# Half of the first layer's output projection moved from behind the HGRN heads to between their levels

## What is computed

```python
proj = hn @ w_in_even[j]
u, q_b, f_b, i_b, g_b = jnp.split(proj, [...], axis=-1)
y_a = s5_mixer(u, ...)                       # (B, L, 512): state space layer and GLU
y_b = hgrn2_mixer(q_b, f_b, i_b, g_b, ...)   # (B, L, 512): 4 heads of 128
h = h + jnp.concatenate([y_a, y_b], axis=-1) @ w_out_even[j]
hn = rms_norm(h, mlp_norm[i])
h = h + jnp.square(jax.nn.relu(hn @ w_mlp_in[i])) @ w_mlp_out[i]
```

## Time and profile before

| | us |
|---|---|
| median of 3 runs | 2602.95 |
| lowest, highest | 2598.78, 2605.69 |
| the profiled execution's own time | 2599.74 |
| its span in the profile | 2598.0 |

### The profile page before, as it was taken

One profiled execution on the slowest core, in us unless ns is written; L12 is line 12 of the kernel. 1 busy time (PEld: TensorE's weight loads), 2 busy tenths in 40 slices (PEclk: granted clock), 3 DMA queues, 4 the chain that ended last, 5 costly groups with the idle time before them and its releaser, 6 DMA issues.

```text
span 2598.0 us, 32798 instructions
## 1 busy us (share of the span) xinstructions
PE 2464.0 (95%) x13054; PEld 1998.5 (77%) x13054; DVE 1191.4 (46%) x1229; ACT 548.1 (21%) x850; POOL 833.8 (32%) x493
## 2 busy tenths in 40 slices
PE   8999946899999999999997999989999999999997
PEld 6887745688888888888885776668888888888885
DVE  6886388432432422424617355652432332424625
ACT  3110424311001011011212145632001001011215
POOL 3421442133333333333322244552333333333321
PEclk9999967999999999999998999999999999999998
DMA  7372421211111111111212211021111111111211
GB/s 209 101 115 73 144 68 34 98 49 49 49 48 48 46 46 48 47 48 48 65 49 85 53 25 57 17 73 49 49 46 47 47 47 48 48 48 49 65 49 65
DMA packets 248296, 159.19 MB, mean 61 GB/s; under 512 B 31524, under 2 KB 235400, under 8 KB 248200
## 3 DMA queue, kind: packets, MB, share of 16 engines
q1 hardware_dynamic: 233224, 133.79, 17.9%
q10 hardware_dynamic: 14992, 24.25, 3.5%
HBM read 131.67 MB, written 25.17 MB: 60 GB/s over the span
## 4 chain that ended last, share of the span: by engine, by line
PE 86%; DVE 9%; issue 2%; ACT 2%; POOL 1%; DMA 0%; ACTq 0%; POOLq 0%; DVEq 0%; SPq 0%
PE ps L596 70%; PE ps L1075 3%; PE ps L747 2%; PE ps L1107 2%; PE ps L1035 1%; DVE hg_queries_keys L1849 1%; PE ps L1048 1%; PE ps L1059 1%; PE ps L663 1%; PE ps L768 1%; DVE stage L1519 1%; ACT x_hi L1158 1%; PE ps L783 1%; DVE s_state L1589 1%; DVE stage L1589 1%
## 5 line engine op out<-in xcount | busy, mean ns | idle before, releaser
L450 POOL CAST w_hi<-w_raw 128x1024 fp32r<-128x1024 f32 x198 | 213.0, 1076 | 1499.6 <-PE ps L596 1222.5
L596 PE MATMUL ps<-x_hi,w_hi 128*128 128x512 f32 x1600 | 496.6, 392 | 6.4 <-issue 3.2
L596 PE MATMUL ps<-x_lo,w_hi 128*128 128x512 f32 x1600 | 493.3, 389 | 0.0
L596 PE MATMUL ps<-x_hi,w_lo 128*128 128x512 f32 x1600 | 493.0, 389 | 0.0
L452 POOL TENSOR_TENSOR w_lo<-w_raw,w_hi 128x1024 fp32r<-128x1024 f32 x198 | 487.7, 2463 | 15.8
L596 PE MATMUL ps<-mid_hi,w_hi 128*128 128x512 f32 x1216 | 376.1, 391 | 8.6 <-DVE mid_lo L1908 5.8
L596 PE MATMUL ps<-mid_lo,w_hi 128*128 128x512 f32 x1216 | 375.3, 390 | 0.0
L596 PE MATMUL ps<-mid_hi,w_lo 128*128 128x512 f32 x1216 | 375.2, 390 | 0.0
L596 PEld LDWEIGHTS ps<-x_hi,w_hi 128*128 128x128 f32 x1600 | 299.9, 188 | 73.2 <-issue 8.8
L596 PEld LDWEIGHTS ps<-x_lo,w_hi 128*128 128x128 f32 x1600 | 300.7, 188 | 62.9
L596 PEld LDWEIGHTS ps<-x_hi,w_lo 128*128 128x128 f32 x1600 | 300.6, 188 | 62.7
(11 more groups left out here) (288 smaller groups left out, 2488.7 us busy)
## 6 DMA issues: line engine op xcount, KB each, us to landing
w_raw<-w_mlp_in_in SPq DMA_DIRECT2D x64, 512.0 KB, 4.0
w_raw<-w_mlp_out_in SPq DMA_DIRECT2D x64, 512.0 KB, 4.0
w_raw<-w_in_even_in SPq DMA_DIRECT2D x20, 512.0 KB, 4.0
residual_dram<-residual ACTq DMA_DIRECT2D x2, 4096.0 KB, 13.0
fqig_dram<-stage ACTq DMA_DIRECT2D x16, 512.0 KB, 2.7
w_raw<-w_ple_gate_in SPq DMA_DIRECT2D x16, 512.0 KB, 4.0
x_tokens<-x_in SPq DMA_DIRECT2D x8, 512.0 KB, 7.3
w_raw<-w_out_even_in SPq DMA_DIRECT2D x8, 512.0 KB, 4.1
```

The lines of the kernel that those rows point to most:

```text
L450: pool.tensor_copy(WH[:, b, :], RAW[:, b, :]).then_inc(S["w_hi_done"], 1)
L596: ins = pe.matmul(acc[:, h, :], w[:, k, :], x[:, k0 + k, h * HALF:(h + 1) * HALF], start=(k == 0 and w is wh and x is xh), stop=(k == kts ...
```

## The change

The projection's weight is now loaded in pieces of 512 rows by 256 columns (`out_half(part, q)`): slabs 22 to 25 are the rows that meet the S5 half, 26 to 29 those of the HGRN half. `out_first` is a generator of the first half's 192 matmuls, for each of 8 output tiles and 2 token halves 12 matmuls into PSUM bank 3; `dense(first, FILL)` runs 4 of them after every half level of heads 1 to 3 and of the tail until none is left. ScalarE copies each finished 12 (`parts`) to a stage buffer and stores it in DRAM. Bank 3 is taken from the transposes and squares, whose two halves now take turns in bank 2, with new waits. POOL prepares slabs 24 to 27 behind the heads. After the heads SP loads residual and stored part tile by tile, 16 DMAs of 512 KB, then slabs 28 and 29; POOL adds the part to the residual (`add_out_part`), and TensorE runs eight units of 24 matmuls.

```diff
@@ -331,14 +336,18 @@
                 sp.wait_ge(S["s5_y_stored"], 16 * L * (k + 1))
                 sp.dma_start(YT[:, k, :], y_dram[k * P:(k + 1) * P, :]).then_inc(yt_loaded[k], 16)
 
-            w = a["w_out_even"][0]
+            def out_half(part, q):
+                src = a["w_out_even"][0][part * HALF:(part + 1) * HALF, q * 256:(q + 1) * 256].rearrange("(k p) n -> p k n", p=P)
+                load(q % 2, SLAB["out"] + 4 * part + q - 1, src)
             tile_of_y(0)
             for s in range(2):
                 src = a["s5_w_glu"][0][:, s * 256:(s + 1) * 256].rearrange("(k p) n -> p k n", p=P)
                 load(s, 20 + s - 1, src)
                 tile_of_y(s + 1)
             tile_of_y(3)
-            load(0, 21, cols(w, slice(0, P)))
+            out_half(0, 0)
 
             for b in range(2):
                 sp.wait_ge(spilled[b], 16 * 10)
...
@@ -361,15 +370,22 @@
                 sp.dma_start(G[:, :], fqig_dram[(hd * 4 + 3) * P:(hd * 4 + 4) * P, :]).then_inc(hg_g_loaded[p], 16)
 
             head_load(0)
-            load(1, 22, cols(w, slice(P, 2 * P)))
+            out_half(0, 1)
             for hd in range(1, HEADS):
                 head_load(hd)
+                if hd < HEADS - 1:
+                    out_half(0, hd + 1)
+            out_half(1, 0)
+            out_half(1, 1)
             sp.wait_ge(S["hg_y_low"], 2 * HEADS)
             sp.wait_ge(S["h_spilled"], 16)
-            sp.dma_start(H[:, :, :], h_dram.rearrange("(k p) t -> p k t", p=P)).then_inc(S["h_restored"], 16)
-            with sp.Fori(1, 4) as i:
-                for b in range(2):
-                    load(b, i * 2 + (22 + b - 1), cols(w, bass.ds(i * 256 + b * P, P)))
+            for b in range(2):
+                sp.wait_ge(spilled[b], 16 * (10 + KT))
+            for m in range(KT):
+                sp.dma_start(H[:, m, :], h_dram[m * P:(m + 1) * P, :]).then_inc(tile_loaded[m], 16)
+                sp.dma_start(OPART[:, m, :], part_dram[m * P:(m + 1) * P, :]).then_inc(tile_loaded[m], 16)
+            out_half(1, 2)
+            out_half(1, 3)
             mlp(SLAB["mlp0"], 0)
             run(SLAB["gate0"], 8, a["w_ple_gate"][0])
             ple_up(SLAB["up0"], 0)
...
@@ -519,9 +535,18 @@
                 if hd < HEADS - 1:
                     queries(hd + 1)
                     gate_scale(hd + 1)
-            with pool.Fori(0, 3) as i:
-                for b in range(2):
-                    split(b, i * 2 + (24 + b + 1), i * 16 + 16 * 13, i * 2 + (26 + b - 1))
+                if hd:
+                    one(SLAB["out"] + hd + 1, 4 * hd, "opart_done")
+            one(SLAB["out"] + 5, 16, "opart_done")
+            def add_out_part(m):
+                pool.wait_ge(tile_loaded[m], 16 * 3)
+                pool.tensor_tensor(H[:, m, :], H[:, m, :], OPART[:, m, :], ALU.add).then_inc(S["out_part"], 1)
+            for m in range(KT):
+                add_out_part(m)
+                if m in (2, 4):
+                    one(SLAB["out"] + 5 + m // 2, UNIT["out"] + m, "acc_done")
             run(SLAB["mlp0"], UNIT["mlp0"], 64)
             run(SLAB["gate0"], UNIT["gate0"], 8)
 
...
@@ -798,7 +823,7 @@
                 glu_part(m, 3).then_inc(S["acc_done"], 1)
 
             pe.wait_ge(S["glu_sig"], 2)
-            NEARS, DIRECT, OB, XB_ = (4, 6), (5, 7), (0, 1), (2, 3)
+            NEARS, DIRECT, OB, XB_ = (4, 6), (5, 7), (0, 1), (2, 2)
 
             def level(hd, l, half):
 
@@ -832,9 +857,11 @@
             def key_tokens(hd, half):
                 u, x = 2 * hd + half, XB_[half]
                 pe.wait_ge(S["hg_update"], (hd + 1) * LEVELS)
+                pe.wait_ge(S["hg_v_copied"], 2 * hd + 2)
                 if hd:
-                    pe.wait_ge(S["hg_ss_read"], u - 1)
-                pe.wait_ge(S["hg_v_copied"], u + 1)
+                    pe.wait_ge(S["hg_ss_read"], 2 * hd)
+                if half:
+                    pe.wait_ge(S["hg_k_copied"], u)
                 for c in range(4):
                     ins = pe.transpose(PS[:, x, c * P:(c + 1) * P], KQ[:, hd % 2, 1, half * HALF + c * P:half * HALF + (c + 1) * P], ident[:, :])
                 ins.then_inc(S["hg_k_tr"], 1)
@@ -842,8 +869,10 @@
             def value_tokens(hd, half):
                 u, x = 2 * hd + half, XB_[half]
                 pe.wait_ge(hg_loaded[hd % 2][half], 48 * (hd // 2 + 1))
-                if hd:
-                    pe.wait_ge(S["hg_k_copied"], u - 1)
+                if hd and half == 0:
+                    pe.wait_ge(S["hg_k_copied"], u)
+                if half:
+                    pe.wait_ge(S["hg_v_copied"], u)
                 for c in range(4):
                     ins = pe.transpose(PS[:, x, c * P:(c + 1) * P], VR[:, hd % 2, half, c * P:(c + 1) * P], ident[:, :])
                 ins.then_inc(S["hg_v_tr"], 1)
@@ -873,15 +902,48 @@
             def head_squares(hd, half):
                 u = 2 * hd + half
                 pe.wait_ge(S["hg_squares"], u + 1)
-                pe.wait_ge(S["hg_v_copied"], min(u + 3, 2 * HEADS))
+                pe.wait_ge(S["hg_v_copied"], min(2 * hd + 4, 2 * HEADS))
+                pe.wait_ge(S["hg_k_copied"], 2 * hd + 2)
+                if half:
+                    pe.wait_ge(S["hg_ss_read"], u)
                 pe.matmul(PS[:, XB_[half], :], ones[:, :], PA[:, half, :], start=True, stop=True).then_inc(S["hg_ss"], 1)
 
+            def out_first():
+                pe.wait_ge(S["mid_ready"], 8)
+                for m in range(KT):
+                    s = SLAB["out"] + m // 2
+                    wh, wl = out_weights(m)
+                    if m % 2 == 0:
+                        pe.wait_ge(S["w_ready"], s + 1)
+                    for h in range(2):
+                        if m + h:
+                            pe.wait_ge(S["opart_copied"], 2 * m + h)
+                        for k in range(4):
+                            for w, x in ((wh, XBh), (wh, XBl), (wl, XBh)):
+                                last = k == 3 and w is wl
+                                ins = pe.matmul(PS[:, 3, :], w[:, k, :], x[:, k, h * HALF:(h + 1) * HALF],
+                                                start=(k == 0 and w is wh and x is XBh), stop=last)
+                                if last:
+                                    ins.then_inc(S["opart_done"], 1)
+                                yield
+            def out_weights(m):
+                return (w[:, m // 2 % 2, :].rearrange("p (k n) -> p k n", n=256)[:, :, m % 2 * P:(m % 2 + 1) * P] for w in (WH, WL))
+            def dense(work, count):
+                for _ in range(count):
+                    next(work, None)
+            first = out_first()
             for hd in range(HEADS + 1):
                 now, tail = hd < HEADS, hd - 1
                 for l in range(LEVELS):
                     for half in range(2):
                         if now:
                             level(hd, l, half)
+                        if hd:
+                            dense(first, FILL)
                         if hd == 0 and l == 3 and half == 1:
                             pe.wait_ge(S["glu_sig"], 4)
                             for other in range(2):
@@ -901,9 +963,14 @@
 
             pe.wait_ge(S["hg_y_low"], 2 * HEADS)
             pe.wait_ge(S["mid_ready"], 8)
-            one(22, 24, XB)
-            one(23, 25, XB)
-            run(24, 26, 6, XB)
+            pe.wait_ge(S["opart_copied"], 16)
+            for m in range(KT):
+                u = UNIT["out"] + m
+                if m % 2 == 0:
+                    pe.wait_ge(S["w_ready"], SLAB["out"] + 4 + m // 2 + 1)
+                pe.wait_ge(*free_of(u - 2))
+                wh, wl = out_weights(m)
+                unit(ACC[m % 2], wh, wl, XBh, XBl, kts=4, k0=4)
 
             def mlp(name, norm, mid0):
                 s, u = SLAB[name], UNIT[name]
...
@@ -1365,32 +1428,57 @@
                     glu_sigmoid(m + 2)
             for half in range(2):
                 value_copy(0, half)
-            for hd in range(HEADS + 1):
+            copied = [0]
+            def parts(hd, slot):
+                while copied[0] < 2 * KT and 12 * (copied[0] + 1) <= FILL * (2 * LEVELS * (hd - 1) + slot + 1):
+                    j = copied[0]
+                    m, h = divmod(j, 2)
+                    o = ST[m % 4][:, h * HALF:(h + 1) * HALF]
+                    act.wait_ge(S["opart_done"], j + 1)
+                    if j == 0:
+                        act.wait_ge(S["mid_ready"], 8)
+                    if m >= 4 and h == 0:
+                        act.wait_ge(spilled[m % 2], 16 * (10 + 4))
+                    fn(o, PS[:, 3, :], ACT.Copy).then_inc(S["opart_copied"], 1)
+                    act.wait_ge(S["opart_copied"], j + 1)
+                    act.dma_start(part_dram[m * P:(m + 1) * P, h * HALF:(h + 1) * HALF], o).then_inc(spilled[m % 2], 16)
+                    copied[0] += 1
+            for half in range(2):
+                forget(1, half)
+            for half in range(2):
```

(56 more changed lines are left out.)

24 lines of the change are left out of this document (12 added, 12 removed).

## The result

The changed kernel took 2610.85 us (median of 8 runs, 2605.08 to 2616.72), the kernel before 2600.86 beside it (8 runs, 2597.55 to 2605.69): ratio 1.0036, 95% interval 1.0021 to 1.0051. The forecast was 2611. The profiled execution took 2608.18 us for a span of 2606.3.

A forecast was written before the change was run, and what follows sets the result against it. Two regimes: in the heads a PE and VectorE chain, from the projection on PE alone. Heads +39 and stage -31 gave +8 on 2602.95, so 2611 us; range 2586 to 2632.

The forecast's parts named there:

- Stage, -31 predicted: Projection's first matmul through mlp0's first unit: 101.0 us before, 70.0 after, giving back 31.0.
- The rival that let the loads land sooner: Projection stage: loads land sooner and norm chain runs as in the later stage; gain 37, total +2, 2605; chance 0.17.
- Heads, +39 predicted: Heads 1 to 3 and tail: added matmuls, copy waits and bank sharing cost 36.3 us at full clock, 39 with clock loss.
- The tail's 3.4: Tail: 24 matmuls, 5.5 us, and a copy gap of 0.8, against 2.83 of existing PE wait: 3.4.
- The 3 us for the clock: Heads and tail: some portions run at 0.43 us a matmul after idle times; 3 us added to 36.3.
- Head 2's copy behind the gates: Head 2, level 4: seventh group's copy stands behind both forget gates and holds PE; 5.3 us with the gates' shift.
- Head 1's copy terms (4.6 and 4.5): Head 1: copy behind gates and a square and value copy, 4.6 us; copy behind table load, Ln and Exp, 4.5.
- Portions between the halves: Levels 1 and 2: each four-matmul portion delays the update by 0.91 us; 7.0 in all with head 3's extras.
- Bank sharing, 2.9 + 4.7: Outputs: first ones matmul waits for second value copy behind two portions; 2.9 us later in head 2, 4.7 in head 3.
- The cover works: Rival: PE's idle time in the heads hides the portions; heads +16, total -18, 2585; chance 0.22 shared with free copies.
- The clock: Rival: new stalls keep PE's clock low in the heads; 19 us on top, total +27, 2630; chance 0.19.
- free copies: Opposite rival: ScalarE's copies do not hold PE; most of 18 us goes, total -10, 2593; shares the 0.22 chance.

The follow-up runs named there:

- experiment 1: Changed kernel with weight slabs 28 and 29 loaded ahead of the sixteen tile loads: 2608.55 us, ratio 1.0042 to the kernel before.
- experiment 2: Changed kernel with slabs 28 and 29 loaded first and GpSimd's eight adds of the stored half left out: 2597.1 us, ratio 0.9991 to the kernel before.
- experiment 5: Three variants of the changed kernel: all 192 matmuls behind the tail, or 84 only between or only behind level halves, rest behind tail: 2637.24, 2625.59, 2619.04 us.
- experiment 6: Changed kernel with the same matmuls placed unevenly, in groups up to twelve, and earlier ScalarE copies: 2593.14 us, ratio 0.9969 to the kernel before.
- experiment 4: Changed kernel without ScalarE's sixteen copies of the sums and PE's waits for them: 2601.26 us, ratio 0.9999 to the kernel before.

## Why the prediction was right

The total and both its large terms held; the terms inside the heads did not all hold, and their errors went both ways.

- **The total, 2611 and 2610.85: part of this closeness is luck.** A difference of 8 was predicted and 10.0 measured. The forecast stood on a median before of 2602.95 (3 runs), where 8 runs give 2600.86: a base 2.1 too high hid a difference 2.0 too small. In the profiles the predicted stretches and the one before head 1 come to +13.1, and 4.8 less behind them, in code that did not change, brought the span back to +8.3.
- **Stage, -31 predicted, -31.4 measured.** Each step is in the trace: slab 28 landed 25.1 us after the start (27.4 predicted), PE stood 5.2 (6), residual 3 at 32.4 (33.3), tiles then 8.2, 8.8, 5.9 and 8.4 us apart (8.2 for each of the next three), end 69.4 (70.0). The last step came out by another path: mlp0's first unit started 57.5 us in, not 59.1, behind the projection's last unit and not behind residual 6, and then waited for tile 7's low half; the two misses nearly cancel. The rival that let the loads land sooner would have changed little, as experiment 1 shows; the contention in the norm chain was dear (experiment 2).
- **Heads, +39 predicted, +42.4 measured.** By stretch 10.9, 10.7 and 14.6 at full clock against 13.0, 11.8 and 17.7. The tail's 3.4 are 3.4 in the trace. The 3 us for the clock were not a term of their own: the granted clock rose in every stretch (0.92, 0.89 and 0.96, from 0.78, 0.65 and 0.89). It is still low at four places of the heads, each behind a time in which PE stood: in head 1 behind 4.5 us (about 415 to 422), in head 2 behind 5.0 (443 to 449) and behind 2.3 (460 to 463), in head 3 behind 2.0 (477 to 480). What it cost at each was not separated.
- **Head 2's copy behind the gates:** 5.3 predicted; a stall of 5.0, level 4 longer by 6.3, and 7.0 back when it is undone.
- **Head 1's copy terms (4.6 and 4.5) are the mis-sized ones.** PE waits for copies there for 3.1 us in all (9.9 in head 2, 5.1 in head 3 and the tail), and leaving all copies out left its stretch at 43.8. That kernel still has the portions and the split beside the block decays (2.9 us that I had put at nothing, as cover of GpSimd's four splits). The places were right: of head 1's +13.0, level 5 has 7.5 (2.9 of it that meeting) and level 6 has 4.0. But without copies these two levels gave back 3.0, not 9.1. The rest is left to the portions, the shared bank and the late ones matmul, without a run that parts them, and the copies' share stays open too: without them the clock was 0.88, update 2 took 3.03, and levels 3 and 4 grew by 2.9, so a gain may have been eaten.
- **Portions between the halves:** the prediction let them count at levels 1 and 2 only (7.0 us in all, with head 3's); experiment 5 shows 7.6 us at these two levels and 14.2 more at levels 3 to 6, where I had put 0.9. In the changed kernel levels 1 and 2 grew by 5.7 in all. So part of what I had priced as copy waits and ones matmuls at levels 4 to 6 was probably this; experiment 5 is another kernel, and no run shows how much.
- **Bank sharing, 2.9 + 4.7:** 2.2 in sum without portions (3.1 at its place). The prediction's terms held portions ahead of the outputs as well; that these are the rest is argued, not shown.
- **Head 3:** level 1 grew by 3.7, where 0.9 for the portion and 0.6 for the copy behind the table load and gate were put down. The copy's stall is 2.0 of it, the portion 0.9, the low clock behind the stall most of the rest. It is the same mechanism as in head 2, at a place where I had read no row.
- **Before head 1:** 2.1 us not in the sum. 1.5 of them lie in head 0: the value transposes wait for a copy out of the shared bank, and VectorE's update after them had 2.4 us idle. The other 0.7 were there before head 0's first update, which comes between 335.8 and 341.2 us in the kernels of this document, with code ahead of it that is nearly the same.
- **Rivals.** "The cover works" did not happen as the change stood, and is possible: experiment 6, with the same matmuls at other places and earlier copies, gains 17.8. "The clock" did not happen. The opposite side, free copies, was right in place and wrong in price: 10.4 of the 18.3 us of copy terms came back (experiment 4), and the time is that of before, not 10 us faster.

## What to carry to other kernels

Ask of a filler not how idle the engine is in sum but what it is next due to do: here 84 matmuls cost 22.6 us between two halves that an update waits for, and 9.6 behind them. Where VectorE was busy anyway (level 0 of heads 2 and 3), even those between the halves cost nothing. A filler's helpers (the copy out of its bank, the split of its weights, its add) each stand in another engine's queue, and there the waits of 2.0 and 5.0 us arose. An operation that is moved to an idle engine is not free if that engine shares memory with the one on the path; the same add, put into a wait of the busy engine, was free as far as a stage of 57.1 us against 57.8 without any adds can tell.

## What the runs showed of the hardware

- A VectorE operation with both operands in SBUF (the memory in which tiles such as `H` lie) takes 1.22 us for 128x1024 float32, and up to 3.42 with GpSimd's adds or splits beside it; six small ones took 4.53 in place of 1.65. The residual's read, with one operand in PSUM, took its 1.23 at 569.72 with a GpSimd add beside it. Here squares that started at 565.69, 0.9 us into a subtraction that ended at 568.02, ended at 569.10, 1.08 later. The Trainium skill ("SBUF — State Buffer", the two separate sides) says that of a VectorE operation with two SBUF inputs and a GpSimd one that reads SBUF, whoever starts first holds the shared port pair for the whole instruction and the other blocks until it ends: on this row the trace agrees, about 1.1 us of the work being done after the other's end. The subtraction before it fits too: it started at 564.77 while x_lo ran until 565.77, and took 3.25 in place of 2.4.
- Eight GpSimd adds (2.4 us each undisturbed, 23.3 in all beside VectorE's work) cost a stage 10.0 us, 7.4 of them in VectorE's chain (experiments 1 and 2).
- After 5.0 us of PE standing still in head 2, the next dense matmuls start 0.43 us apart, the lower of the two levels, and are at 0.23 again by 450.4. With more portions in heads 1 and 2 the clock was higher: 0.76 and 0.75 granted without them (experiment 5), 1.00 and 0.96 with 56 a head (experiment 6).
- When groups of twelve follow each other in one PSUM bank, the handshake costs PE 1.0 us a group (copy 0.60 and the two hand-overs; experiment 5).
